# A decoder layer in split fp32: one more pair by seven products, with paced GpSimd sums and six weight slots

## The reference

```python
    h = rmsnorm(x, g_ffn_pre[l])
    ff = (jax.nn.silu(h @ w_gate[l]) * (h @ w_up[l])) @ w_down[l]
    x = x + rmsnorm(ff, g_ffn_post[l])
```

## Time and profile before

| | |
|---|---|
| time, median of 3 runs | 1206.5 us (1206.4 to 1206.55) |
| the profiled execution's own time | 1206.21 us |
| its span, first to last instruction | 1204.5 us |
| busy in the span | PE 1191.2, DVE 936.3, ACT 678.0, POOL 214.4 us |
| mean granted TensorE clock | 0.998 |
| DMA | 230.67 MB, mean 192 GB/s |

### The profile page before, as it was taken

How to read it: one execution, slowest core, us unless ns; L and a number is a source line. 1 busy time by engine, 2 the same in 40 slices (tenths; PEclk the granted TensorE clock), 3 DMA queues, 4 the chain that set the end, 5 groups by cost and what they waited for, 6 DMA issues and landing times.

```text
span 1204.5 us, 16367 instructions
## 1 busy us (share of the span) xinstructions
PE 1191.2 (99%) x5760; PEld 998.0 (83%) x5760; DVE 936.3 (78%) x1230; ACT 678.0 (56%) x896; POOL 214.4 (18%) x158
## 2 busy tenths in 40 slices
PE   8999999999999999999999999999999999999997
PEld 7888888888888888888888888888888878888885
DVE  6657877877777755777888888788888788879887
ACT  5654676475554645655556555555655555556553
POOL 1000200000000000004323333422433123313320
PEclk9999999999999999999999999999999999999999
DMA  8657867767686565454665556566456665554552
GB/s 316 208 151 159 227 174 168 177 133 214 165 198 190 189 206 181 169 187 163 210 210 196 183 184 233 181 206 211 165 186 208 231 218 203 196 201 165 206 197 97
DMA packets 122723, 230.67 MB, mean 192 GB/s; under 512 B 8104, under 2 KB 24752, under 8 KB 122032
## 3 DMA queue, kind: packets, MB, share of 16 engines
q1 hardware_dynamic: 122208, 226.85, 60.9%
q0 software_dynamic: 464, 3.15, 0.6%
HBM read 227.88 MB, written 2.11 MB: 191 GB/s over the span
## 4 chain that ended last, share of the span: by engine, by line
PE 94%; DVE 3%; ACT 1%; DMA 1%; issue 0%; POOL 0%; SPq 0%; DVEq 0%; ACTq 0%
PE bank L1713 93%; PE bank L1990 1%; DMA resid<-in_x 1%; DVE w_lo L1068 1%; DVE gT L1282 0%; PE bank L1718 0%; PE bank L1907 0%; ACT w_hi L657 0%; DVE gT L1278 0%; DVE h L1095 0%; DVE w_lo L1554 0%; DVE pre L1260 0%; DVE resid L1706 0%; ACT w_hi L977 0%; DVE pre L1255 0%
## 5 line engine op out<-in xcount | busy, mean ns | idle before, releaser
L1713 PE MATMUL bank<-w_hi,h2T 128*128 128x512 f32 x1126 | 359.3, 390 | 0.0
L1068 DVE TENSOR_TENSOR w_lo<-raw,w_hi 128x1024 fp32r<-128x1024 f32 x172 | 209.3, 1224 | 119.8 <-ACT w_hi L657 119.0
L1554 DVE TENSOR_TENSOR w_lo<-raw,w_hi 128x1024 fp32r<-128x1024 f32 (+1 forms) x164 | 215.8, 1320 | 74.0 <-ACT w_hi L977 72.8
L657 ACT ACTIVATE w_hi<-raw 128x1024 fp32r<-128x1024 f32 x172 | 180.8, 1058 | 160.4 <-PE bank L1713 146.1
L1713 PE MATMUL bank<-hT,w_hi 128*128 128x512 f32 x768 | 270.9, 396 | 0.0
L977 ACT ACTIVATE w_hi<-raw 128x1024 fp32r<-128x1024 f32 (+1 forms) x164 | 156.3, 954 | 168.0 <-PE bank L1713 141.9
L1713 PEld LDWEIGHTS bank<-w_hi,h2T 128*128 128x128 f32 x1126 | 211.4, 188 | 44.0
L1713 PE MATMUL bank<-hT,w_lo 128*128 128x256 f32 x768 | 214.6, 279 | 0.0
L1713 PE MATMUL bank<-w_lo,h2T 128*128 128x512 f32 x543 | 211.3, 389 | 0.0
L1551 DVE TENSOR_TENSOR w_lo<-raw,w_hi 128x1024 fp32r<-128x1024 f32 x166 | 197.8, 1223 | 15.9 <-ACT w_hi L966 14.4
L966 ACT ACTIVATE w_hi<-raw 128x1024 fp32r<-128x1024 f32 x166 | 170.0, 1055 | 67.2 <-PE bank L1713 64.9
(11 more groups left out here) (232 smaller groups left out, 1261.9 us busy)
## 6 DMA issues: line engine op xcount, KB each, us to landing
raw<-in_w_in SPq DMA_DIRECT2D x63, 1024.0 KB, 10.8
raw<-in_w_down SPq DMA_DIRECT2D x88, 512.0 KB, 5.2
raw<-in_w_up SPq DMA_DIRECT2D x80, 512.0 KB, 4.0
raw<-in_w_gate SPq DMA_DIRECT2D x80, 512.0 KB, 4.8
raw<-in_w_out SPq DMA_DIRECT2D x16, 1024.0 KB, 5.1
raw<-in_w_gate SPq DMA_DIRECT2D x4, 1024.0 KB, 5.2
raw<-in_w_up SPq DMA_DIRECT2D x4, 1024.0 KB, 5.8
resid<-in_x SPq DMA_DIRECT2D x2, 1024.0 KB, 7.1
```

The lines of the kernel that those rows point to most:

```text
L657: act.activation(part_of(w_hi, rnd, s), src, ACT.Copy).then_inc(hi_done, 1)
L1068: dve.tensor_tensor(part_of(w_lo, rnd, s), raw_sub(rnd, s)[1], part_of(w_hi, rnd, s).bitcast(F32), ALU.subtract).then_inc(lo_done, 1)
L1554: dve.tensor_tensor(slot_blocks(w_lo, slot, piece), seven_blocks(piece, q), slot_blocks(w_hi, slot, piece).bitcast(F32), ALU.subtract)\
L1713: return pe.matmul(out_, lhsT, rhs, start=start, stop=stop, skip_group_check=True)
```

## The change

The plans get more S pairs: in groups 1 to 9 pairs 2, 3, 5 and 6 instead of 2, 4 and 6, in group 10 pairs 2 and 3 instead of 2 and 4, in each half of w_down eight of 22 instead of six. POOL keeps only t3; the two other sums become one DVE instruction behind piece 1. In the groups, POOL's sums get waits: the first for the first lo of the group, the second for the third lo, the third for the first pair's new DVE instruction, the fourth for the last lo of pair 3. There are six weight slots instead of four (the last eight pieces of w_down use four). Their memory is taken from `resid`, which is written to DRAM ahead of group 1 and read back when PE has eight pieces left.

```diff
-SEVEN = (2, 4, 6)
+SEVEN = (2, 3, 5, 6)
+FF_SLOTS = 6
+END_SUBS = 8
...
-FULL = Plan("RRSRSRSR")
-FINAL = Plan("RRSRSRRR")
-DOWN = Plan("RRRSRRSRRSRRSRRSRRSRRR")
-LAST_HALF = Plan("RRSRRSRRSRRSRRSRRSRRRR")
+FULL = Plan("RRSSRSSR")
+FINAL = Plan("RRSSRRRR")
+DOWN = Plan("RRRSRSRRSRSRRSRSRRSRSR")
+LAST_HALF = Plan("RRSRSRSRSRRSRSRSRSRRRR")
...
+def slot_depth(i, m, first=False):
+
+    return AHEAD if at_end(i, m) or (first and m < AHEAD) else FF_SLOTS
...
@@ sync
+            sp.wait_ge(resid_ready, TT * CHUNKS)
+            for t in range(TT):
+                sp.dma_start(resid_rows.ap()[t * P:(t + 1) * P, :], resid[:, t, :]).then_inc(spilled, 16)
             for n in range(4):
                 unit_rows(1, n, FF_FIRST - 8 + FREE[n])
...
+            sp.wait_ge(sub_done, N_SUBS - END_SUBS)
+            sp.wait_ge(spilled, 16 * TT)
+            for t in range(TT):
+                sp.dma_start(resid[:, t, :], resid_rows.ap()[t * P:(t + 1) * P, :]).then_inc(resid_back, 16)
...
@@ gpsimd
-            def weight_sums(i, n, plan):
-
-                q, made = chunk_of(i, n), sums_index(i, n)
-                b12, b22, b11, b21 = (raw[:, q, 512 * c:512 * (c + 1)] for c in range(4))
+            def up_sum_of(i, n):
+
+                q = chunk_of(i, n)
+                b12, b22 = raw[:, q, 0:512], raw[:, q, 512:1024]
                 pool.wait_ge(raw_up[q], up_arrived(i, n))
                 pool.tensor_tensor(b12, b22, b12, ALU.subtract).then_inc(t3_ready, 1)
-                pool.wait_ge(t2_ready, made + 1)
-                pool.tensor_tensor(b22, b22, b11, ALU.subtract).then_inc(t14_ready, 1)
-                pool.wait_ge(lo_done, ff_base(i) + (plan.base[n] + 2))
-                pool.tensor_tensor(b21, b21, b11, ALU.subtract).then_inc(t14_ready, 1)
+
+            def first_pairs_sums(i):
+
+                pool.wait_ge(lo_done, ff_base(i) + 1)
+                up_sum_of(i, SEVEN[0])
+                pool.wait_ge(lo_done, ff_base(i) + 3)
+                up_sum_of(i, SEVEN[1])
 
             with pool.Fori(1, FF_GROUPS - 1) as i:
-                for n in SEVEN:
-                    weight_sums(i, n, FULL)
-            for n in SEVEN[:2]:
-                weight_sums(FF_GROUPS - 1, n, FINAL)
+                first_pairs_sums(i)
+                pool.wait_ge(t14_ready, sums_index(i, SEVEN[0]) + 1)
+                up_sum_of(i, SEVEN[2])
+                pool.wait_ge(lo_done, ff_base(i) + FULL.base[SEVEN[1] + 1])
+                up_sum_of(i, SEVEN[3])
+            first_pairs_sums(FF_GROUPS - 1)
...
                 for n in DOWN_SEVEN[half]:
-                    weight_sums(FF_GROUPS + half, n, DOWN_PLANS[half])
+                    up_sum_of(FF_GROUPS + half, n)
...
@@ scalar, unit_hi
-                act.wait_ge(sub_done, ff_base(i) + (m - 3))
+                if first and m >= AHEAD and m < FF_SLOTS:
+                    act.wait_ge(spilled, 16 * TT)
+                act.wait_ge(sub_done, ff_base(i) + (m + 1 - slot_depth(i, m, first)))
...
-                    act.wait_ge(t14_ready, 2 * sums_index(i, n) + 2)
+                    act.wait_ge(t14_ready, sums_index(i, n) + 1)
...
@@ vector, unit_lo
+                elif piece == 1:
+                    dve.wait_ge(lo_done, ff_base(i) + (m + 1))
+                    dve.wait_ge(t2_ready, sums_index(i, n) + 1)
+                    pair = raw[:, q, :].rearrange("p (a c) -> p a c", c=512)[:, 1::2, :]
+                    dve.tensor_tensor(pair, pair, raw[:, q, 1024:1536].unsqueeze(1).to_broadcast([P, 2, 512]),
+                                      ALU.subtract).then_inc(t14_ready, 1)
...
@@ vector, ahead of group 1 and at the end
                 lo(R_FF + 1, s + AHEAD)
-                if s:
-                    seven_sums(s - 1)
+                seven_sums(s)
...
+                if t == 0:
+                    dve.wait_ge(resid_back, 16 * TT)
```

More of the change, by code:

```diff
@@ L137, in sums_index, with at_end, ff_slot @@
     if down_half(i) is not None:
-        return 3 * FF_GROUPS - 4 + HALF_SEVEN * down_half(i) + DOWN_SEVEN[down_half(i)].index(n)
-    return 3 * i + (SEVEN.index(n) - 3)
+        return len(SEVEN) * (FF_GROUPS - 2) + 2 + HALF_SEVEN * down_half(i) + DOWN_SEVEN[down_half(i)].index(n)
+    return len(SEVEN) * i + (SEVEN.index(n) - len(SEVEN))
 def sum_banks(odd):
     return (4, 0) if odd else (0, 4)
-def ff_slot(i, odd, m):
+def at_end(i, m):
+    return isinstance(i, int) and i == FF_GROUPS + 1 and m >= DOWN.subs - END_SUBS
+def ff_slot(i, m):
+    if at_end(i, m):
+        return m % AHEAD
     if down_half(i) is not None:
-        return (ff_base(i) + m) % AHEAD
-    return (m + (0 if odd else FULL.subs)) % AHEAD
+        return (ff_base(i) + m - FF_FIRST) % FF_SLOTS
+    return m % FF_SLOTS
+def slot_depth(i, m, first=False):
+    return AHEAD if at_end(i, m) or (first and m < AHEAD) else FF_SLOTS
 def event_of(rnd, unit):
@@ L230, in hybrid_layer @@
         w_lo = sb("w_lo", [P, AHEAD, SUB], F32R)
-        resid = sb("resid", [P, TT, D])
+        resid_home = ExitStack()
+        resid = sb("resid", [P, TT, D], stack=resid_home)
+        resid_home.close()
+        more_hi = sb("more_hi", [P, FF_SLOTS - AHEAD, SUB], F32R)
+        more_lo = sb("more_lo", [P, FF_SLOTS - AHEAD, SUB], F32R)
+        resid_rows = nc.dram_tensor("resid_rows", (SEQ, D), F32)
         columns = sb("columns", [P, 2, P])
@@ L309, in s_upper @@
         def s_upper(j):
-            return s_hi[:, j] if j < 2 else s_third[:, 0]
+            return s_hi[:, j] if j < 2 else (s_third, s_fourth)[j - 2][:, 0]
         def s_lower(j):
-            if j == 2:
-                return s_third[:, 1, 0:2, :], s_third[:, 1, 2:4, :]
+            if j >= 2:
+                lower = (s_third, s_fourth)[j - 2]
+                return lower[:, 1, 0:2, :], lower[:, 1, 2:4, :]
             return s_lo12(j), s_lo34[:, j]
@@ L322, in seven_blocks @@
             return (blocks[:, 1:3, :], blocks[:, 3:4, :], blocks[:, 0::2, :], blocks[:, 1::2, :])[piece]
+        hi_slots = [w_hi[:, s, :] for s in range(AHEAD)] + [more_hi[:, s, :] for s in range(FF_SLOTS - AHEAD)]
+        lo_slots = [w_lo[:, s, :] for s in range(AHEAD)] + [more_lo[:, s, :] for s in range(FF_SLOTS - AHEAD)]
+        early_hi_slots = [early[:, 0, s, :] for s in range(AHEAD)]
+        early_lo_slots = [early[:, 1, s, :] for s in range(AHEAD)]
         def slot_blocks(w, slot, piece):
-            return w[:, slot, :].rearrange("p (a c) -> p a c", c=512)[:, 0:1 if piece == 1 else 2, :]
+            return w[slot].rearrange("p (a c) -> p a c", c=512)[:, 0:1 if piece == 1 else 2, :]
         def s_lo12(j):
@@ L406, in hybrid_layer @@
         resid_ready = sem("resid_ready")
+        spilled = sem("spilled")
+        resid_back = sem("resid_back")
         h_ready = sem("h_ready")
@@ L990, in ff_group @@
                         first_product(i - 1, FULL, c0)
-                    unit_hi(i, odd, plan, m)
+                    unit_hi(i, odd, plan, m, first)
                     if m == 0 and first:
-                        act.wait_ge(s_summed, 3)
-                        for j in range(3):
+                        act.wait_ge(s_summed, len(SEVEN))
+                        for j in range(len(SEVEN)):
                             act.activation(s_upper(j), s_sum[:, j], ACT.Copy).then_inc(s_rounded, 1)
@@ L1593, in ff_group @@
                     unit_lo(i, odd, plan, m)
-                    if first and 1 <= m < 4:
+                    if first and 1 <= m <= len(SEVEN):
                         seven_lo(m - 1)
@@ L1757, in wide_columns, with sub_tokens @@
                         after(s)
-            def sub_tokens(count, slot, act_T, pair, k0, last, tiles=range(TT), w_hi=w_hi, w_lo=w_lo):
+            def sub_tokens(count, slot, act_T, pair, k0, last, tiles=range(TT), w_hi=hi_slots, w_lo=lo_slots):
                 pe.wait_ge(lo_done, count)
@@ L1766, in sub_tokens @@
                         lo_x = act_T[:, k, SEQ + t * P:SEQ + (t + 1) * P]
-                        mm(bank[:, 2 * pair + t, :], hi_x, w_hi[:, slot, w], k == 0, False)
-                        mm(bank[:, 2 * pair + t, :], hi_x, w_lo[:, slot, w], False, False)
-                        ins = mm(bank[:, 2 * pair + t, :], lo_x, w_hi[:, slot, w], False, k == last)
+                        mm(bank[:, 2 * pair + t, :], hi_x, w_hi[slot][:, w], k == 0, False)
+                        mm(bank[:, 2 * pair + t, :], hi_x, w_lo[slot][:, w], False, False)
+                        ins = mm(bank[:, 2 * pair + t, :], lo_x, w_hi[slot][:, w], False, k == last)
                 if TT - 1 in tiles:
@@ L2059, in ff_group @@
                     if plan.units[n] == "R":
-                        sub_tokens(ff_base(i) + (m + 1), ff_slot(i, odd, m), h2T, c0 // 2 + 1 - piece, 2 * n, KT - 1)
+                        sub_tokens(ff_base(i) + (m + 1), ff_slot(i, m), h2T, c0 // 2 + 1 - piece, 2 * n, KT - 1)
                         if m == 2:
@@ L2064, in ff_group @@
                         if n == SEVEN[0] and piece == 0:
```

(4 more changed lines are left out.)

38 lines of the change are left out of this document (19 added, 19 removed).

## The result

| | before | after |
|---|---|---|
| time, median (lowest to highest) | 1206.57 us (1206.4 to 1210.08, 6 runs) | 1211.22 us (1210.44 to 1213.09, 6 runs) |
| ratio after/before, 95% interval | | 1.0035 [1.0024, 1.0046] |
| the profiled execution's own time, span | 1206.21, 1204.5 us | 1210.44, 1208.7 us |
| transposes of one group to those of the next, groups 1 to 9 | 42.52 to 42.64 us | 42.80 to 42.86 us, the first 43.26 |
| from the start of the last transposes to PE's end | 225.96 us | 227.55 us |

The kernel became 0.35% slower: 4.65 us by the medians, 4.2 by the two spans. Forecast was 2.7 faster. The time lies inside the whole range (1196 to 1212), outside the forecast's own (1201 to 1207), and close to rival C's 1211.8, but for another reason than C's.

What follows compares the result with a forecast made beforehand. TensorE was taken as the bound (1191 of 1204.5 us busy). Groups -3.1, first half of w_down -2.3, second half +2.7 sum to -2.7: 1206.21 to 1203.5, as a median 1203.8; range 1196 to 1212, the forecast's own 1201 to 1207.

Steps and rivals of the forecast that it cites:

- rival C: Groups: one of GpSimd's first three sums, the first, meets a DVE lo, period 43.16, total 1211.8; chance 0.24.
- The mechanism of the groups: Groups 1 to 9: DVE becomes the bound by a little; period 42.61 to 42.26, nine giving -3.1 us.
- sums 1 to 3: GpSimd's first three sums per group: covered, costing DVE 0, 0.13 and 0.12 at most.
- the fourth: GpSimd's last sum per group: meets the lo's of plain pair 4 and costs DVE 1.09.
- An S pair is then 5.97: Groups: DVE time of one S pair, 1.25 + 0.61 + 0.72 + 3 x 1.13, against 4.77 on PE.
- 0.07: Groups: wait of an S pair's last lo on DVE for ACT's rounding, 0.07 us.
- the loop of the prediction: Groups: DVE from transposes to pair 6's third lo 25.92, then 72 PE matmuls 16.34; together a period of 42.26.
- The new subtraction: DVE instruction making two sums at once: 1.13 from start to start, 1.22 to its end.
- DVE's own sum, 42.07: DVE's work in one group: 40.73 plus 0.13, 0.12 and 1.09 of GpSimd sums, against 41.71 for PE.
- First half of w_down: Matmuls -1.36 and 0.9 of a 1.10 wait at the first S won: -2.3 us.
- Second half: w_down: plain + S 11.23 on DVE, 10.22 on PE; PE waits 4.8 in all, net +2.7 us.
- Other edits: resid's spill and reload, and a fourth set of token sums before group 1: taken at 0.

Runs made afterwards that it cites:

- Experiment 8: The changed kernel with its eight S pairs in the second half of w_down at 3, 5, 7, 9, 11, 13, 15, 17: 1209.77 us.
- experiment 1: The changed kernel with the fourth GpSimd sum of groups 1 to 9 (pair 6) made by DVE itself: 1207.5 us.
- experiment 4: The changed kernel with three S at pairs 2, 4, 6 and four slots in the groups, and seven spread S in w_down's second half: 1201.44 us.
- experiment 7: The changed kernel with the first weight sum of each S pair in w_down's second half made by DVE instead of GpSimd: 1210.44 us.
- experiment 2: The changed kernel with four weight slots instead of six everywhere, same plans: 1230.82 us.

## Why the prediction was wrong

**The mechanism of the groups was right, its size was not.** DVE became the bound; PE waits where it was said, 0.45 of idle before pair 6's third piece; sums 1 to 3 are covered, the fourth costs 1.12 (taken: 1.09); pairs 0 and 1 with the extras take 11.03 (11.02). The step that failed is the size of an S pair on DVE, "An S pair is then 5.97" and "0.07" of wait: 6.04 taken, 6.14 to 6.23 measured, with the same fault in pair 2. Measured against taken, on DVE:

| | taken | measured |
|---|---|---|
| pair 2, with the transposed lo | 7.31 | 7.55 |
| pair 3 | 6.04 | 6.23 |
| pair 4 | 3.36 | 3.39 |
| pair 5 | 6.04 | 6.21 |
| pair 6 | 6.04 | 6.14 |
| pairs 0, 1, 7 | 13.28 | 13.30 |
| DVE in one group | 42.07 | 42.82 |

(Pair 3 begins where its t2 at 722.42 stands, less 1.34.) Three pieces make 0.65 of the 0.75; the rest are steps of 0.01 to 0.03. First, from piece 0 to t2 it takes 1.34, 1.34, 1.33 and 1.26, where 1.25 was taken for all: +0.27. The trace of before had told this piece. Its three S pairs in a group show 1.34, 1.25 (the row) and 1.37, of which these are the two others:
```profile
594.86 1.21 DVE L1554 TENSOR_TENSOR w_lo<-raw,w_hi 128x1024 fp32r<-128x1024 f32 x1
596.20 0.69 DVE L1562 TENSOR_TENSOR raw<-raw 128x512 f32<-128x512 f32 x1
...
628.12 0.69 DVE L1562 TENSOR_TENSOR raw<-raw 128x512 f32<-128x512 f32 x1
```
I took the least of three for the groups, and 1.33 for w_down. Their mean, 1.32, would have brought the loop of the prediction to 42.47, still 0.14 under the old period: it does not turn the sign alone. Second, the last two lo of an S take 2.41 (734.50 to 736.91) where 2.33 was taken, ACT's rounding being later by that: +0.08 in each of three pairs. Third, the transposed lo starts 1.32 behind the subtraction of pair 2, not 1.13, because it waits for ACT's rounding of the turned result, which starts 1.18 behind the transposes (716.74, 715.56), as it did before: +0.14 with its own length. The new subtraction itself, which no row showed, was right: 1.22 long, 1.14 to the next start.

The loop "to 42.26" closes as drawn, with these sizes in it: 42.84 from transposes to transposes (715.56 to 758.40 in the timeline, 0.17 later in the chain). Pairs 3 and 5 give 0.36 of the 0.58, and PE 0.15, with 16.49 instead of 16.34 for the 72 matmuls behind its wait. That the transposed lo waits shows that this loop and DVE's own work close together. So the nine periods gave +2.4, not -3.1. DVE's own sum, 42.07, is made of some forty steps, and stood 0.36 from PE's 41.71: too near to tell the sign from rows that scatter by 0.1. The text said that 0.5 of DVE work beyond the sum would turn it, and 0.75 did. It named the wrong candidate: rival C's sum 1 stays covered (1.30 at 704.23), and C's time came from elsewhere; that it fits is luck. By C's own numbers the sum was covered: 0.6 late and 1.3 long, it ends 0.7 ahead of the next lo, as it does in the trace (705.53, lo at 706.27).

Which part of the 1.34 is a semaphore and which is ACT or GpSimd is not separated by any run.

**First half of w_down: right.** -2.3 taken; 9.30 to the first S against 13.56 before, less 15 matmuls (3.40), is 0.86 of wait won (0.9 was taken), and the 408 matmuls behind it run without a wait: -1.36 - 0.86 = -2.2. (The text's "four matmul triples" are two; its 6 x 0.2269 is right.)

**Second half: right in mechanism, 1.1 larger.** Taken +2.7 with 4.8 of PE waits; by difference +3.8 (1.59 + 2.2). Waits of 0.6 at 1095.31 and 3.1 at 1105.35 make 3.7, the half clock 1.8 more, which no step had; against that stand the -1.36 of the matmuls and the 0.7 of before, so the sum is known to some 0.4. Experiment 8, with another order of the pairs, shows the sum itself: plain + S 11.23 taken, 11.13 measured; 4.8 of loss taken, 4.6 measured.

By the Trainium skill ("SBUF — State Buffer", Who interferes with whom) a DVE instruction with two SBUF inputs contends with a GpSimd instruction that reads SBUF. The trace agrees: in experiment 8 L1609 takes 2.21 with a sum beside it, 1.22 without one in the changed kernel (716.20), and GpSimd's sum 3.17 instead of 1.30. The price of one such meeting in this kernel is thus 0.99, and 1.12 in experiment 1.

**Other edits: right at nothing for `resid`, short for the token sums.** No wait of PE, ACT or DVE on the spill or the reload of `resid` is on the chain. The fourth set of token sums was taken at 0. The lo of its result takes 0.67 of DVE in pair 2 of group 1:
```profile
543.55 0.75 DVE L1583 TENSOR_TENSOR s_fourth<-s_sum,s_fourth 128x256 fp32r<-128x256 f32 x2
```
The first period is 43.26, 0.4 over the other eight; in experiment 4, which has three sets, it is 42.41 like the rest. No run tests the one as the cause of the other.

## What to carry over

Where a change moves work from the bounding engine to one with a sixth of its time to spare, write down both engines' sums for one period: a gain of 0.68 us per S is there only while DVE's sum stays below PE's (36.96 of 40 us busy still cost nothing, 39.23 cost more than the S saved). When such sums differ by less than the scatter of the rows that they are made of, take the mean of all like rows and not one, and let the chances show that the sign is open. Here a sum given to GpSimd was free beside DVE operations that read PSUM; beside those with two SBUF inputs it cost DVE 1.12, and DVE made it itself for 0.67.

## What the runs showed of the hardware

- Behind 2.92 us of PE idle the granted clock went to 0.50 for 3.41 us in the changed kernel (and to the same level behind 2.88 in experiment 1), but it stayed at 1.00 behind 2.76 in experiment 7 and behind 2.94 in experiment 2. What decides is not shown.
- Behind a wait PE's next step is slow at full clock too: at 741.91 the second matmul follows after 0.34 and the ten behind it after 0.232 on average; in the group of 186 that waits for nothing it is 0.2269.
- GpSimd's 512 sum took 1.30 beside DVE operations that read PSUM, 2.22 beside one DVE lo and 4.17 beside several short DVE operations with SBUF inputs (1099.44 in the changed kernel).
